# PEER experts as dense, once-streamed products in place of gathered rows, in a two-layer decoder trunk

## The reference, cut to what matters

```python
qry = (x_blk @ w_query).reshape(T, 8, 2, 128)
scores = jnp.einsum('thpd,hpnd->thpn', qry, sub_keys)
top_s, top_i = lax.top_k(scores, 16)
cand_s = (top_s[:, :, 0, :, None] + top_s[:, :, 1, None, :]).reshape(T, 8, 256)
cand_i = (top_i[:, :, 0, :, None] * 128 + top_i[:, :, 1, None, :]).reshape(T, 8, 256)
best_s, best_pos = lax.top_k(cand_s, 16)
idx = jnp.take_along_axis(cand_i, best_pos, axis=-1)
gate = jax.nn.softmax(best_s, axis=-1)
act = jax.nn.gelu(jnp.einsum('thkd,td->thk', expert_u[idx], x_blk))
out = jnp.einsum('thk,thkd->td', gate * act, expert_v[idx])
```

## Time and profile before

| what | us |
|---|---|
| median of 3 runs (1577.03 to 1577.71) | 1577.28 |
| profiled execution, first to last instruction (its span) | 1573.6 |
| PE / DVE / ACT / POOL busy | 1359.1 / 974.8 / 672.1 / 577.9 |
| mean granted TensorE clock | 0.976 |

### The profile page before, as it was taken

The page is one execution under the profiler, slowest core; times in us unless marked ns, Lnnn a source line. Parts: engine busy times, 40 slices in busy tenths (PEclk is TensorE's granted clock), DMA queues, the critical chain, the costliest instruction groups (busy, mean ns, idle before and its releaser), DMA issues.

```text
span 1573.6 us, 15026 instructions
## 1 busy us (share of the span) xinstructions
PE 1359.1 (86%) x4096; PEld 658.3 (42%) x4096; DVE 974.8 (62%) x2433; ACT 672.1 (43%) x1917; POOL 577.9 (37%) x534
## 2 busy tenths in 40 slices
PE   7999998889777988889989699788999878787776
PEld 5555565444322433334555244334465422232222
DVE  3327598988774344764477765566556888554544
ACT  2324443434344234873434333586443434443433
POOL 1001565654442333343333234334433433343331
PEclk9999999999999999999999899999999999999999
DMA  9317999999999999999999999999999999999996
GB/s 377 150 54 294 399 412 421 421 421 421 421 421 421 422 421 421 421 421 421 421 421 422 387 423 422 421 412 398 421 421 420 421 421 421 422 422 421 421 422 250
DMA packets 85523, 620.42 MB, mean 394 GB/s; under 512 B 10401, under 2 KB 10401, under 8 KB 11969
## 3 DMA queue, kind: packets, MB, share of 16 engines
q0 software_dynamic: 75056, 551.65, 84.6%
q1 hardware_dynamic: 9792, 67.51, 10.4%
q10 hardware_dynamic: 592, 0.31, 0.1%
HBM read 618.38 MB, written 1.05 MB: 394 GB/s over the span
## 4 chain that ended last, share of the span: by engine, by line
PE 40%; DMA 37%; ACT 9%; DVE 9%; issue 4%; POOL 1%; SPq 0%; ACTq 0%; DVEq 0%; POOLq 0%
DMA arena<-in_peer_uv_dram,hnT 25%; PE banks L550 25%; PE banks L577 6%; PE banks L430 5%; DMA work<-in_peer_uv_dram,hnT 5%; DMA raw<-in_peer_uv_dram,hnT 3%; ACT g_e L934 2%; DVE arena L1440 2%; DMA rt<-in_diff_lambda_k_dram 2%; DMA spare<-in_peer_uv_dram,hnT 2%; PE banks L698 2%; PE banks L522 1%; ACT L971 1%; ACT hnT L926 1%; DVE raw L1440 1%
## 5 line engine op out<-in xcount | busy, mean ns | idle before, releaser
L550 PE MATMUL banks<-arena,g_e 128*128 128x512 f32 x1184 | 584.9, 622 | 113.8 <-ACT g_e L934 112.9
L341 POOL DMA_INDIRECT arena<-in_peer_uv_dram,hnT x297 | 320.8, 1080 | 512.6 <-PE banks L550 496.8
L550 PEld LDWEIGHTS banks<-arena,g_e 128*128 128x128 f32 x1184 | 214.5, 195 | 400.7 <-ACT g_e L934 210.2
L923 ACT ACTIVATE hnT<-hnT 128x1 f32<-128x1 f32 x512 | 103.4, 202 | 631.6 <-DVE hnT L1440 629.7
L1440 DVE CUSTOM_DVE_ANT_0 arena<-arena,hrows 128x1024 f32<-128x1024 f32 x209 | 254.0, 1222 | 169.6 <-DMA arena<-in_peer_uv_dram,hnT 169.5
L550 PE MATMUL banks<-raw,g_e 128*128 128x512 f32 x424 | 205.8, 612 | 27.9 <-ACT g_e L934 26.1
L934 ACT ACTIVATE g_e<-ident,hnT 128x128 f32<-128x128 f32 x501 | 201.2, 402 | 46.5 <-ACT hnT L926 0.7
L341 POOL DMA_INDIRECT raw<-in_peer_uv_dram,hnT x106 | 117.4, 1107 | 154.2 <-PE banks L550 150.3
L926 ACT ACTIVATE hnT<-hnT,arena 128x1 f32<-128x1 f32 x512 | 150.8, 294 | 52.1 <-DVE arena L1627 5.5
L1440 DVE CUSTOM_DVE_ANT_0 arena<-arena,banks 128x1024 f32<-128x1024 f32 x90 | 109.7, 1220 | 84.6 <-DMA arena<-in_peer_uv_dram,hnT 84.4
L1440 DVE CUSTOM_DVE_ANT_0 raw<-raw,hrows 128x1024 f32<-128x1024 f32 x80 | 97.4, 1222 | 59.1 <-DMA raw<-in_peer_uv_dram,hnT 59.1
(11 more groups left out here) (251 smaller groups left out, 1260.8 us busy)
## 6 DMA issues: line engine op xcount, KB each, us to landing
arena<-in_diff_in_dram SPq DMA_DIRECT2D x24, 1024.0 KB, 9.4
arena<-in_peer_query_dram SPq DMA_DIRECT2D x16, 1024.0 KB, 9.4
arena<-in_gla_in_dram POOLq DMA_DIRECT2D x5, 2048.0 KB, 21.5
arena<-in_peer_query_dram SPq DMA_DIRECT2D x4, 2048.0 KB, 9.3
arena<-in_diff_out_dram SPq DMA_DIRECT2D x8, 1024.0 KB, 9.2
arena<-in_peer_uv_dram,hnT POOLq DMA_INDIRECT x301, 20.2
work<-in_gla_out_dram POOLq DMA_DIRECT2D x2, 2048.0 KB, 40.3
arena<-in_gla_in_dram SPq DMA_DIRECT2D x2, 1024.0 KB, 11.5
```

Of the source, the lines that this page charges most:

```text
L341: pool.indirect_dma_start(pair(n), None, table, bass.IndirectOffsetOnAxis(ap=places[:, o:o + 1].bitcast(u32), axis=0)).then_inc(S(f"pair_l ...
L550: last = nc.tensor.matmul(bank(2 * (tile % NT) + half), diags[:, slot * P:(slot + 1) * P], v_row(n)[:, half * 512:(half + 1) * 512], start ...
L923: A(acts[:, o:o + 1], dots[:, o:o + 1], ACT.Gelu).then_inc(S("gelu_done"), 1)
```

## The change

The expert mixer reads no single rows any more. For each layer both tables are read once from front to back, in 128 blocks of 512 KB each, and every expert is computed for all 256 tokens; a matrix that is zero for the experts that a token did not pick does the choosing.

- *Tables.* On the host u is laid out so that block j holds the 128 experts with second index j, transposed (`peer_u_t`), and v by the same blocks (`peer_v_t`). SP streams u's blocks, then v's, through a ring of six slots of 4 KB a partition; a load waits until the block that had its slot is used (`block_used`). All indirect transfers, the dots, the diagonal matrices and the tick schedule go.
- *Up.* `up_pair`: for a block, 8 products of 256 columns, u's block as weights, the normed tokens transposed (`hn2T`) as columns; two blocks to a bank, four banks. ACT's `pair_out` writes the gelu of a bank to `blocks`, a 128 KB a partition array over (j, token).
- *Gates.* DVE searches as before, all lists of a layer during the first up pairs; the lists of the first index, the second index and the gate are turned (`lists_turned`), so that slots stand on partitions. For a token, a 128x128 product of two matrices of ones and zeros, one of them scaled by the gates, is the gate of every expert: DVE compares an iota with the lists (`ones_at`), POOL multiplies by the gates, PE multiplies four tokens to a bank (`group`), and DVE multiplies the bank into the up products that are there already and copies the rest (`group_out`); later pairs are multiplied in by `pair_mixed`. Groups go three to a pair from pair 38 on.
- *Down.* Per block four products of 512 columns, `blocks` as weights, v's block as columns, into four banks.
- *Rest.* `layer1` now runs alone between the two expert layers, both tiles interleaved, diff weights loaded once (during the first down) and its second query weights behind them. The gain of the feed-forward norm is applied after the transposes. GLA's weights are loaded by SP, not POOL.

```diff
-            for n in range(ROWS - APART):
...
-                pool.indirect_dma_start(
-                    pair(n), None, table,
-                    bass.IndirectOffsetOnAxis(ap=places[:, o:o + 1].bitcast(u32), axis=0)
-                    ).then_inc(S(f"pair_loaded_{HOME[n]}"), 16)
+            for s in range(STREAMED):
...
+                elif s >= R:
+                    sp.wait_ge(S("block_used"), s - R + 1)
+                load(s)
+                n, over = divmod(s - R + 1 - BLOCKS, 8)
+                if over == 0 and 1 <= n <= 16:
+                    load_mixer(n - 1)
...
+            for layer in range(LAYERS):
+                for g in range(GROUPS):
...
+                    pool.wait_ge(S("hot"), layer * GROUPS + g + 1)
+                    one = hot[g % 4][0].rearrange("p (q i) -> p q i", q=QUAD)
+                    gate = turned_lists[:, 2, QUAD * g:QUAD * (g + 1)].unsqueeze(2).broadcast_to([P, QUAD, P])
+                    pool.tensor_tensor(one, one, gate, ALU.mult).then_inc(S("weighted"), 1)
...
+            def up_pair(layer, n):
+
+                if n >= 4:
+                    pe.wait_ge(S("pairs_out"), layer * PAIRS + n - 3)
...
+                for j in range(2 * n, 2 * n + 2):
+                    s = stream(layer, 0, j)
+                    wait_landed(pe, s)
+                    for k in range(KD):
+                        last = nc.tensor.matmul(dst[:, j % 2 * SEQ:(j % 2 + 1) * SEQ], slot(s)[:, k * P:(k + 1) * P],
+                                                hn2T[:, k, :], start=(k == 0), stop=(k == KD - 1))
+                    last.then_inc(S("block_used"), 1)
...
+            def group(layer, g):
+
+                if g == 0:
+                    pe.wait_ge(S("lists_out"), layer * NT + NT)
+                if g >= 4:
+                    pe.wait_ge(S("groups_out"), layer * GROUPS + g - 3)
+                pe.wait_ge(S("weighted"), layer * GROUPS + g + 1)
+                for q in range(QUAD):
+                    last = nc.tensor.matmul(bank(g % 4)[:, q * P:(q + 1) * P], hot[g % 4][0][:, q * P:(q + 1) * P],
+                                            hot[g % 4][1][:, q * P:(q + 1) * P], start=True, stop=True)
+                last.then_inc(S("spread"), 1)
+
+            def down(layer):
...
+                    for half in range(2):
+                        last = nc.tensor.matmul(bank(2 * m + half), ar(j * SEQ + m * P, P),
+                                                slot(s)[:, half * 512:(half + 1) * 512],
+                                                start=(j == 0), stop=(j == BLOCKS - 1))
...
+                places = iota[:].unsqueeze(1).broadcast_to([P, QUAD, P])
+                for c in range(2):
+                    of = turned_lists[:, c, QUAD * g:QUAD * (g + 1)].unsqueeze(2).broadcast_to([P, QUAD, P])
+                    last = V.tensor_tensor(hot[g % 4][c].rearrange("p (q i) -> p q i", q=QUAD), places, of, ALU.is_equal)
+                last.then_inc(S("hot"), 1)
+
+            def group_out(layer, g):
+
+                n = 2 * PAIRS_BEFORE[g]
+                dve.wait_ge(S("spread"), layer * GROUPS + g + 1)
+                dve.wait_ge(S("pairs_out"), layer * PAIRS + PAIRS_BEFORE[g])
+                src = bank(g % 4).rearrange("p (q j) -> p q j", q=QUAD)
+                dst = blocks_tj[:, QUAD * g:QUAD * (g + 1), :]
+                last = V.tensor_tensor(dst[:, :, 0:n], dst[:, :, 0:n], src[:, :, 0:n], ALU.mult)
+                if n < BLOCKS:
+                    last = V.tensor_copy(dst[:, :, n:], src[:, :, n:])
+                last.then_inc(S("groups_out"), 1)
+
+            def pair_mixed(layer, n):
+
+                i, t = MIXED.index(n), QUAD * GROUPS_BEFORE[n]
+                dve.wait_ge(S("pairs_out"), layer * PAIRS + n + 1)
+                dve.wait_ge(S("groups_out"), layer * GROUPS + GROUPS_BEFORE[n])
+                dst = blocks_jt[:, 2 * n:2 * n + 2, 0:t]
+                V.tensor_tensor(dst, dst, tmp(i)[:, :, 0:t], ALU.mult).then_inc(S("mixed_out"), 1)
...
+                for kind, n in EVENTS:
+                    if kind == "group":
+                        if n + AHEAD < GROUPS:
+                            ones_at(layer, n + AHEAD)
+                        group_out(layer, n)
+                    elif kind == "pair" and n in MIXED:
+                        pair_mixed(layer, n)
```

More of the change, by code:

```diff
@@ L96 @@
[L96 to L121, removed]
@@ L124 @@
[L124 to L139, removed]
+LAYERS = 2
+BLOCKS = NK
+PAIRS = BLOCKS // 2
+QUAD = 4
+GROUPS = SEQ // QUAD
+LAST = 4
+LISTS_AT = (20, 37)
+EXPS_AT = (15, 34)
+AHEAD = 3
@@ L194, in trunk_kernel @@
[L194 to L206, removed]
@@ new lines, in trunk_kernel, with weights, stream, slot @@
+        R = len(slots)
+        def weights(n):
+            return S(f"weights_loaded{n % 16}")
+        def stream(layer, phase, j):
+            return (2 * layer + phase) * BLOCKS + j
+        def slot(s):
+            return slots[s % R]
+        def wait_landed(engine, s):
+            engine.wait_ge(S(f"slot_loaded{s % R}"), 16 * (s // R + 1))
+        blocks_jt = arena[:].rearrange("p (j t) -> p j t", t=SEQ)
+        blocks_tj = arena[:].rearrange("p (j t) -> p t j", t=SEQ)
+        hot = [[wk(W_HOT + (2 * g + c) * BANK, BANK) for c in range(2)] for g in range(4)]
@@ L261, in load_halves @@
[L261 to L271, removed]
@@ L362, in _, with wait_weights @@
         @block.tensor
         def _(pe):
+            def wait_weights(n):
+                pe.wait_ge(weights(n), landed(n))
             def scale_rows():
@@ new lines, in lists_turned @@
+            def lists_turned(layer, m):
+                pe.wait_ge(S("settled"), layer * NT + m + 1)
+                for c in range(3):
+                    last = nc.tensor.transpose(bank(m)[:, c * P:(c + 1) * P], listed(m, c), ident[:])
+                last.then_inc(S("lists_turned"), 1)
+            def group(layer, g):
[8 more added lines that the diff above has]
+                last.then_inc(S("spread"), 1)
@@ L584, in turn, with experts @@
+            def experts(layer):
+                for kind, n in EVENTS:
+                    if kind == "pair":
+                        up_pair(layer, n)
+                    elif kind == "lists":
+                        lists_turned(layer, n)
+                    else:
+                        group(layer, n)
+                down(layer)
             def turn(src, b, done):
@@ new lines, in head_scores @@
+            def head_scores(m, hh):
+                n = m * DH + hh
+                if hh:
+                    pe.wait_ge(S("s_evicted"), n)
+                for half in range(2):
+                    r0 = half * DDH
+                    last = nc.tensor.matmul(
+                        bank(6 + half)[:, 0:(m + 1) * P],
+                        x1(X_QT[m], hh * P, P)[r0:r0 + DDH, :],
+                        keys_of(hh, (m + 1) * P)[r0:r0 + DDH, :],
+                        start=True, stop=True)
+                last.then_inc(S("s_done"), 1)
@@ L1119, in _ @@
             V = nc.vector
-            chain = 0
+            chain = roots = 0
             def link(ins):
```

1594 lines of the change are left out of this document (736 added, 858 removed).

## The result

The changed kernel takes **2340.42 us** (median of 4 runs, 2339.48 to 2340.99) against 1577.15 for the kernel before: 1.484 times as long, 95% interval 1.4823 to 1.4865. The forecast was 1421 and faster.

The account below looks back on a forecast made before the run. Gathered bytes bounded the old kernel, 1275 of 1573.6 us; PE would bound the new one: opening 173, two expert layers of 528, mixer 178, end 10, span 1417, so 1421 us. Forecast band 1385 to 1465, range 1340 to 1510.

Parts of the forecast that it names:

- PE prices: Matmul prices from the opening's dense runs: 0.218 us for 256 columns, 0.434 for 512, 0.117 for 128.
- the opening: Work before the first expert layer's pair 0, dense on PE at the end: about 173 us.
- Bytes, bound and stream: Whole kernel: HBM bytes fall to some 322 MB, PE becomes the bound, the table stream costs nothing.
- The 301 GB/s of the forecast: Stream rate needed in the expert layers: a 512 KB block per 1.74 us; plain loads had run at 398 GB/s.
- Lists: DVE's searches, 17 us per two-head list, 136 for eight; second tile ready near 120 us, wanted at 133: no stall.
- The excess of 52 us a layer: Group stage, pairs 38 to 59: 159 us, 52 more than PE needs, as PE waits for DVE and POOL.
- The step's 2.57: Group stage: time per group in us, DVE's own 2.16 plus 0.41 lost to POOL; bounds 2.16 and 3.32.
- the 0.41 charged for POOL: Group stage: remainder of POOL's 1.17 us gate product after `group_out`'s 0.75, charged as lost to DVE's next comparison.
- Rival 3: Strided `group_out` bounds the layer: step 4.0 us, 1595 in all; slower than now above 2.0 us; chance 0.06.
- Rivals 1 and 2: Group stage: POOL beside DVE costs nothing, step 2.16, 1371 us, chance 0.18; or runs in series, 3.32, 1513, 0.16.
- Mixer: Layer 1's mixer between the expert layers: products plus latencies of head chains 168 us, with slow PE restarts 178.
- The range: Total time of the changed kernel: 1340 to 1510 us, leaving out parts of the rivals.

Follow-up runs that it names:

- run 1: Changed float32 kernel with the second half of the output columns left out of `down` for blocks 1 to 126, both layers: 1909.7 us.
- Run 2: Changed float32 kernel loading only the first six table blocks, later products using stale blocks: 2341.82 us.
- run 3: Changed float32 kernel with both operands of the up products read as the upper 16 bits (bfloat16, cut off): 1871.34 us.
- run 4: Kernel of run 3 with both operands of `down` also read as the upper 16 bits: 1365.97 us, 0.8667 of the kernel before.
- run 5: Kernel of run 4 with the gate product's second operand read from the iota and its output in contiguous scratch, without the 1 KB stride: 1346.78 us.
- run 8: Kernel of run 4 with POOL's product by the gates cut from 512 to 128 columns: 1361.2 us.
- run 7: Kernel of run 5 with POOL's product by the gates cut from 512 to 128 columns: 1305.77 us.

## Why the prediction was wrong

- **The step that failed is "PE prices".** "112 matmuls of 256 columns in 24.44 us, 0.218 us each" is right for a record, and the next sums, "1024 x 0.218" and "512 x 0.434", multiply it by products of the program. For a float32 product it is 0.432 and 0.858 us (kernel after, run 1). Of the 921 us by which the span is over the forecast, 435 are `down`, 388 the two up stages, 44 the opening (the eight queries alone went from 30 to 58) and 55 the mixer; the end gave back 2. Around the span lay 1.7 us (2339.48 against 2337.8), not 3.7.
- **It stood in the trace of before.** The chain shows L550 x4 for a slot, and a slot has two products. L550 also has 424, 200 and 196 records beside the 1184 of the earlier trace rows: 2004 for 501 slots of two products. The prediction wrote "four matmuls of 2.00 us" and "two matmuls of 0.6 us" for the same line and passed on. The page of the kernel before:

```profile
L550 PE MATMUL banks<-raw,g_e 128*128 128x512 f32 x424 | 205.8, 612 | 27.9 <-ACT g_e L934 26.1
...
L550 PE MATMUL banks<-work,g_e 128*128 128x512 f32 x200 | 97.6, 613 | 19.1 <-ACT g_e L934 18.9
L550 PE MATMUL banks<-spare,g_e 128*128 128x512 f32 x196 | 97.6, 622 | 10.2 <-ACT g_e L934 10.1
```

- **Bytes, bound and stream: right.** 323.74 MB for 322, PE over 9 tenths, the records at their forecast pace. Run 2 shows the stream free, at the 134 to 188 GB/s that the expert stages asked of it. The 301 GB/s of the forecast were asked for only where the products had 16-bit operands (runs 3 and 4); there the stream did bound, at 403 to 412 GB/s in run 4, near the 398 of the earlier trace rows.
- **Lists: right, but hardly tested**: PE has no wait for the turned lists in the kernel after, where a pair of 6.91 us in place of 3.49 gave the lists twice the time. Run 4 is the harder test: with a pair in about 2.56 us PE waits 2.6 us for them in all (L518, 2 waits).
- **The group stage.** The excess of 52 us a layer did not appear in the kernel after, because a late pair with three groups keeps PE 6.91 + 3 x 0.94 = 9.7 us and DVE's three steps with their `pair_mixed` some 3 x 155.6/64 = 7.3 (run 4). Where PE was fast enough for DVE to bound, in run 4, the stage took 155.6 us against the forecast's 159. The step's 2.57 was near its 2.43, by two errors that offset each other: the strided product and copy take 1.1 us a step, not 0.75, and the 0.41 charged for POOL is nothing, since the longer product covers POOL's 1.04.
- **Rival 3 (stride).** "I take full pace" from the earlier trace rows was wrong. The groups of DVE by form, in the kernel after (L1576 with the stride, L1587 without):

```profile
L1576 DVE TENSOR_TENSOR arena<-arena,banks 128x472 f32<-128x472 f32 x6 | 7.3, 1210 | 0.0
...
L1587 DVE TENSOR_TENSOR arena<-arena,work 128x512 f32<-128x512 f32 x8 | 5.5, 692 | 48.9 <-ACT work L944 48.9
...
L1576 DVE TENSOR_TENSOR arena<-arena,banks 128x312 f32<-128x312 f32 x6 | 5.1, 848 | 49.1 <-PE banks L526 49.1
```

  (1210 - 848)/(472 - 312) = 2.3 ns an element, against 0.9 in the short clearing. The same view of run 5, the product without the gap (L1581) and the copy (L1583), which reads its bank without a gap and only writes with 1 KB between elements:

```profile
L1581 DVE TENSOR_TENSOR work<-iota,banks 128x472 f32<-128x472 f32 x6 | 3.8, 631 | 0.0
...
L1583 DVE COPY arena<-banks 128x200 f32<-128x200 f32 x6 | 3.0, 501 | 0.0
...
L1581 DVE TENSOR_TENSOR work<-iota,banks 128x312 f32<-128x312 f32 x6 | 2.8, 473 | 4.3 <-PE banks L529 4.3
...
L1583 DVE COPY arena<-banks 128x104 f32<-128x104 f32 x6 | 2.0, 326 | 0.0
```

  That is 1.0 ns an element without the gap and 1.8 with it in the write alone. The rule of the Trainium skill, page "Advanced Engine Details and Errata", section "SBUF Cachelines", that the prediction set aside is borne out. It was still not what decided: the product and copy took 0.35 us more than forecast, and the step did not get longer than its 2.57. Rival 3's threshold was also too low by its own sum: a product and copy of 1.17 us or more leave nothing of POOL's 0.41, so a step of 2.57 + 1.28 = 3.85 us asks for 3.85 - 1.28 - 0.13 = 2.4 us of them, not 2.0.
- **Rivals 1 and 2 (POOL beside DVE).** Each holds for one pair of operations: nothing lost beside the product out of PSUM (run 8), 0.40 us lost of 0.54 together beside a comparison (run 5). The Trainium skill, page "SBUF — State Buffer", section "SBUF: two separate sides", says that a DVE operation with two SBUF inputs and a GpSimd operation that reads SBUF lock each other out, and that the one which started first goes through. The comparison has two such inputs, the product out of PSUM one; the runs agree in which pair loses time, and POOL's product, which had started first, keeps its 1.04 us. The other order stands in run 4 where the stage begins: six comparisons follow each other, and two of POOL's products start while one of them runs. DVE's timeline, then POOL's:

```profile
309.31 5.39 DVE L1569 TENSOR_TENSOR work<-iota,work 128x512 f32<-128x512 f32 x6
```

```profile
310.76 1.35 POOL L313 TENSOR_TENSOR work<-work 128x512 f32<-128x512 f32 x1 [307.18 <-DVE work L1569]
312.74 1.42 POOL L313 TENSOR_TENSOR work<-work 128x512 f32<-128x512 f32 x1 [0.63 <-DVE work L1569]
```

  There both lose: POOL's products take 1.35 and 1.42 us instead of 1.04, and the six comparisons 5.39 us, where run 7 with POOL's short product has 4.11.
- **Mixer.** Its PE work is 212 us, not the 55.6 + 30 + 15 = 100.6 of the forecast, so most of the latencies that the forecast added one by one lie under products; 21 us of the 233 are left without PE.
- **The range** missed because every rival varied waits around PE's work, and none the work.

With these float32 products the plan cannot come under 1577 us: two layers of `up_pair` and `down` alone take 2 x (64 x 6.91 + 439.5) = 1764 us at the measured pace. No run tried another way to form them exactly.

## What to carry to other kernels

Before a duration from a trace is multiplied by a count from the program, count the same line in both: the records of a line, divided by the products that it issues, are a factor of the price. A change that trades bytes for dense products stands or falls with the type of the operands; here the same dense plan is 1.48 times the time before in float32 and 0.87 in 16 bits. And an operation that is made shorter may uncover a neighbour: look what ran beside it.

## What the runs showed that was not expected

- A float32 product is two records of 0.216 us for 256 columns; a 16-bit one is a single record of 0.114. A float32 transpose is one record (the turns of `hn2`, eight in 1.04 us, are x8).
- The upper halves of float32 words can be read in place as 16-bit operands, with a step of two, at that 0.114: no cast, no extra pass (run 3).
- DVE with 1 KB between elements: 2.3 ns an element where a product reads and writes with the gap, 1.8 where the copy only writes with it, 1.0 for the product without it. So the write costs by itself; what the read would cost alone is in no run.
- DVE's comparison and POOL's product get in each other's way: a comparison that comes second loses 0.40 of 0.54 us together (run 5), a product of POOL that comes second takes 1.35 to 1.42 us instead of 1.04 (run 4). DVE's product out of PSUM and POOL's do not.
